# FFN down of layer 1 by seven half-size products, and output products inside the state chain

## What is computed

```python
def conv_ffn(h, p):
    u = dwconv3(h @ p['ffn_up'], p['ffn_conv'])
    ug, uv = jnp.split(u, 2, axis=-1)
    return (jax.nn.silu(ug) * uv) @ p['ffn_down']        # (512, 2816) @ (2816, 1024)

def step(S, inp):                                        # rwkv_scan: both directions, 16 heads
    rt, wt, kt, vt, at, bt = inp
    sa = jnp.einsum('dbhvk,dbhk->dbhv', S, at)
    S = S * wt[..., None, :] + sa[..., :, None] * bt[..., None, :] + vt[..., :, None] * kt[..., None, :]
    y = jnp.einsum('dbhvk,dbhk->dbhv', S, rt) if emit else None
    return S, y
```

## Time and profile before

| | |
|---|---|
| three runs | 2727.85, 2722.11, 2727.54 us (median 2727.54) |
| profiled execution | 2725.52 us, its span 2723.7 us |
| PE busy | 2659.0 us, 98% of the span |
| DVE, ACT, POOL busy | 1398.4, 745.2, 214.9 us |
| granted clock of PE | 0.995 over the span |

### The profile page before, as it was taken

How to read it: one execution, slowest core, us unless ns; L and a number is a source line. 1 busy time by engine, 2 the same in 40 slices (tenths; PEclk the granted TensorE clock), 3 DMA queues, 4 the chain that set the end, 5 groups by cost and what they waited for, 6 DMA issues and landing times.

```text
span 2723.7 us, 61664 instructions
## 1 busy us (share of the span) xinstructions
PE 2659.0 (98%) x27175; PEld 1710.8 (63%) x27175; DVE 1398.4 (51%) x2723; ACT 745.2 (27%) x1566; POOL 214.9 (8%) x184
## 2 busy tenths in 40 slices
PE   7999999999999999999999999999999999999999
PEld 3455555556454545748888544666666677787887
DVE  2677676674222223337778211777877643314541
ACT  3244333442222222111111002443444322311110
POOL 1000000000000002214444000000000000000000
PEclk9999999999999999999999999999999999999999
DMA  7211111111343432344543224212222244356554
GB/s 267 61 48 44 51 51 45 51 48 43 116 116 93 116 111 67 95 130 142 155 124 115 72 72 142 75 53 58 59 60 55 55 124 109 106 153 179 151 149 121
DMA packets 500010, 264.55 MB, mean 97 GB/s; under 512 B 42865, under 2 KB 493889, under 8 KB 499233
## 3 DMA queue, kind: packets, MB, share of 16 engines
q1 hardware_dynamic: 498016, 251.58, 31.9%
q0 software_dynamic: 1728, 9.03, 0.9%
HBM read 255.33 MB, written 5.24 MB: 96 GB/s over the span
## 4 chain that ended last, share of the span: by engine, by line
PE 95%; DVE 2%; DMA 1%; ACT 1%; issue 1%; SPq 0%; DVEq 0%; ACTq 0%
PE psum L515 36%; PE psum L517 15%; PE psum L1190 12%; PE psum L1302 8%; PE psum L549 2%; PE psum L785 2%; PE psum L1019 1%; PE psum L895 1%; PE psum L1007 1%; PE psum L590 1%; PE psum L997 1%; PE psum L758 1%; PE psum L771 1%; PE psum L873 1%; PE psum L731 1%; PE psum L909 1%
## 5 line engine op out<-in xcount | busy, mean ns | idle before, releaser
L515 PE MATMUL psum<-hT,strips 128*128 128x256 f32 (+1 forms) x2234 | 695.0, 462 | 2.4 <-DMA strips<-in_w_in_dram 1.8
L515 PEld LDWEIGHTS psum<-hT,strips 128*128 128x128 f32 x2234 | 414.5, 190 | 228.2 <-issue 192.5
L517 PE MATMUL psum<-hT,strips 128*64 128x512 f32 (+1 forms) x1932 | 403.5, 537 | 4.4 <-DVE arena L2551 2.4
L1302 PE MATMUL psum<-arena,strips 128*128 128x512 f32 (+1 forms) x704 | 227.6, 486 | 0.6 <-DVE arena L2834 0.6
L517 PEld LDWEIGHTS psum<-hT,strips 128*64 128x64 f32 x1932 | 120.9, 137 | 119.4 <-issue 97.6
L1302 PEld LDWEIGHTS psum<-arena,strips 128*128 128x128 f32 x704 | 133.7, 190 | 93.0 <-issue 83.2
L515 PE MATMUL psum<-arena,strips 128*128 128x256 f32 (+1 forms) x416 | 125.9, 461 | 0.9 <-DVE done L2683 0.9
L2834 DVE SCALAR_TENSOR_TENSOR arena<-psum,mod,arena 128x256 f32<-128x256 f32 x24 | 10.9, 481 | 193.7 <-PE psum L1302 193.7
L515 PEld LDWEIGHTS psum<-arena,strips 128*128 128x128 f32 x416 | 78.9, 190 | 45.0 <-issue 36.8
L2216 DVE TENSOR_SCALAR arena<-arena 128x512 f32<-128x512 f32 (+1 forms) x88 | 69.0, 784 | 71.5 <-ACT arena L2068 69.4
L1846 ACT ACTIVATE arena<-psum,arena 128x512 f32<-128x512 f32 (+1 forms) x96 | 58.2, 615 | 151.3 <-DVE arena L2588 151.3
(11 more groups left out here) (306 smaller groups left out, 4110.8 us busy)
## 6 DMA issues: line engine op xcount, KB each, us to landing
strips<-in_w_in_dram SPq DMA_DIRECT2D x152, 512.0 KB, 3.9
strips<-in_ada_w_dram SPq DMA_DIRECT2D x80, 512.0 KB, 4.0
strips<-in_ffn_up_dram SPq DMA_DIRECT2D x46, 512.0 KB, 3.8
strips<-in_ffn_down_dram SPq DMA_DIRECT2D x32, 512.0 KB, 3.9
conv_branch<-in_ffn_up_dram SPq DMA_DIRECT2D x28, 512.0 KB, 4.9
arena<-in_ada_w_dram SPq DMA_DIRECT2D x4, 2048.0 KB, 13.0
strips<-in_w_in_dram SPq DMA_DIRECT2D x32, 256.0 KB, 3.5
strips<-in_a_out_w_dram SPq DMA_DIRECT2D x16, 512.0 KB, 4.5
```

The costliest lines, as they stand in the source:

```text
L515: return pe.matmul(o, lhs, rhs, start=start, stop=stop, skip_group_check=True)
L517: ins = pe.matmul(o[64 * h:64 * h + 64], lhs[:, 64 * h:64 * h + 64], rhs, start=start, stop=stop, skip_group_check=True)
L1302: ins = mm(s.o[:, lo:T], strip[:, b, j, :], hid[:, k, lo:T], k == 0, k == FT - 1)
```

## The change

In layer 1, FFN down is done for pairs of outputs `q`. The first 16 of the 22 blocks of rows go by seven half-size products for each of two groups of eight blocks, summed over the groups in PSUM; the last six blocks (`rest`) are plain matmuls over 512 columns. The pair buffers, the strip sums on POOL and the token sums (now of `hid`) are those of FFN up, with eight more pairs. Layer 2's parameters are turned after the fourth output instead of the third. In both layers the output products of a chunk are issued in the state chain, right behind that chunk's `state_in` and `state_out`; the last chunk's value products stay at the end. The diff, cut:

```diff
--- before.py
+++ after.py
-ALL_PAIRS = LATE_PAIRS + [("up", i) for i in range(1, FT)]
+ALL_PAIRS = LATE_PAIRS + [("up", i) for i in range(1, FT)] + [("down", j) for j in range(D // P)]
...
-PAIR_LOADS = {"gate": 2, "branch": 8, "up": 2}
+FIRST_DOWN = LATE + FT
+SUMMED = 16
+PAIR_LOADS = {"gate": 2, "branch": 8, "up": 2, "down": 2}
...
+        hid_sums = [[arena[:, n:n + 2 * T].rearrange("p (k t) -> p k t", k=4) for n in u] for u in (
+            (AR1_at + 2 * T, after_up), (after_up + 2 * T, after_up + 4 * T),
+            (after_sums + 2 * T, after_sums + 4 * T), (after_up + 6 * T, after_sums))]
+        down_t = arena[:, (n := after_sums + 6 * T):n + T].rearrange("p (j t) -> p j t", j=2)
...
+                fresh = [True, True]
+                def output_bank(i):
+                    if ("y", l, i) not in slots:
+                        take(A, "y", l, i)
+                        fresh[:] = [True, True]
+                    return slots["y", l, i].o
+                def outputs_of_state(c, i):
+                    for d in range(2) if c >= max(c0, 1) else ():
+                        t, back = place(c, d)
+                        for h in range(2):
+                            pe.matmul(output_bank(i)[rows(h), t], GG[rows(h), c, d, :], AR[i % 2][d][rows(h), c, 1, back],
+                                      start=fresh[h], stop=False, skip_group_check=True)
+                            fresh[h] = False
+                def outputs_of_values(c, i):
+                    if c == NCH - 1:
+                        pe.wait_ge(*slots[f"in{c}", l, i].freed)
+                    for d in range(2) if c >= c0 else ():
+                        t, back = place(c, d)
+                        for h in range(2):
+                            ins = pe.matmul(output_bank(i)[rows(h), t], RV[:, c, d, h, :],
+                                            EE[:, 1, c // 4, d, h, c % 4, back], start=fresh[h], stop=True,
+                                            skip_group_check=True)
+                            fresh[h] = False
+                    if c == NCH - 1:
+                        ins.then_inc(slots["y", l, i].full[0], 1)
...
@@ -1169,17 +1188,17 @@
                         state_in(c, i)
                         if c in (1, 2):
                             through_inverse(i, ahead, c + 1)
-                        if c == NCH - 1:
-                            outputs_of_states(i)
-                            if ahead:
-                                diagonal_blocks(i + 1)
+                        outputs_of_state(c, i)
+                        if c == NCH - 1 and ahead:
+                            diagonal_blocks(i + 1)
                         if c > 0:
                             fill(steps, hop)
                         if c < NCH - 1:
                             state_out(c, i)
+                            outputs_of_values(c, i)
                             fill(steps, hop)
                     fill(steps, everything)
-                    outputs_of_values(i)
+                    outputs_of_values(NCH - 1, i)
...
+            def paired_down(q):
+                c, x = slice(0, SEG), slice(SEG, T)
+                ps = down_pairs(q)
+                s, cc = take(Q, "down", 0, 2 * q), take(A, "down11", q)
+                b0 = BANK_P[s.b]
+                u, y, z = PS[:, b0, c], PS[:, b0 + 1, c], PS[:, b0 + 1, x]
+                w2, free = [], []
+                def rest(n):
+                    r = take(G, "rest", n)
+                    pe.wait_ge(*rg.full())
+                    for j in range(FT - SUMMED):
+                        if n == 0:
+                            pe.wait_ge(ev["hid_ready"], SUMMED + j + 1)
+                        ins = mm(r.o, strip[:, rg.last[0], j, :], hid[:, SUMMED + j, :], j == 0, j == FT - SUMMED - 1)
+                        if j == 0:
+                            pay(ins)
+                    ins.then_inc(r.full[0], 1)
+                    owed[0] = rg.free
+                def of_sums(o, j, v, first):
+                    for g, p in enumerate(ps):
+                        pe.wait_ge(ev["strip_sums"], sums_no(p, j + 1))
+                        ins = product(o, strip_sums[p % 2][j], v[g], first and g == 0)
+                        if j == 3:
+                            owed[0] = ev["sums_used"]
+                    return ins
+                for g in range(2):
+                    pe.wait_ge(*pr_w.full(PAIR_LOADS["down"]))
+                    w2.append(pair_w[pr_w.last[0]])
+                    free.append(pr_w.free)
+                    if q == 0:
+                        pe.wait_ge(ev["hid_ready"], 8 * g + 8)
+                    ins = product(u, w2[g][:, 0, 0:4], hid[:, 8 * g:8 * g + 4, c], g == 0)
+                ins.then_inc(ev["down1_ready"], 1)
+                for g in range(2):
+                    ins = product(cc.o[:, c], w2[g][:, 0, 4:8], hid[:, 8 * g + 4:8 * g + 8, c], g == 0)
+                ins.then_inc(cc.full[0], 1)
+                rest(2 * q)
+                if q == 0:
+                    pe.wait_ge(ev["token_sums"], 14)
+                of_sums(y, 0, hid_sums[0], True).then_inc(ev["down5_ready"], 1)
+                pe.wait_ge(ev["down1_kept"], q + 1)
+                if q == 0:
+                    pe.wait_ge(ev["token_sums"], 16)
+                of_sums(u, 1, hid_sums[1], False).then_inc(ev["down6_ready"], 1)
+                pe.wait_ge(ev["down5_kept"], q + 1)
+                if q == 0:
+                    pe.wait_ge(ev["token_sums"], 18)
+                for g in range(2):
+                    pe.wait_ge(ev["strip_sums"], sums_no(ps[g], 4))
+                    product(z, w2[g][:, 1, 4:8], hid_sums[3][g], False)
+                    owed[0] = free[g]
+                pe.wait_ge(ev["down6_kept"], q + 1)
+                if q == 0:
+                    pe.wait_ge(ev["token_sums"], 20)
+                of_sums(u, 2, hid_sums[2], False).then_inc(ev["down7_ready"], 1)
+                of_sums(y, 3, [hid[:, 8 * g + 4:8 * g + 8, x] for g in range(2)], False).then_inc(s.full[0], 1)
+                rest(2 * q + 1)
             def ffn(l, lo):
                 def up(i, j):
@@ -1290,7 +1373,11 @@
                                 for _ in strip_steps(A, up(i, j), lo, hT):
                                     pass
                                 ada_between(4 * i + j)
-                for i in range(KT):
...
-                    if (l, i) == (0, 2):
-                        turn_params(1)
...
+                    elif kind == "down":
+                        sp.dma_start(v[:, q], wcols(a["ffn_down"][0], (n // 2 * 2 + q) * P, 8, n % 2 * 8)).then_inc(pr_w.full(), 16)
...
-                for i in range(KT):
+                for q in range(KT // 2 if l == 0 else 0):
+                    for p in down_pairs(q):
+                        load_pair(p)
+                    for i in range(2 * q, 2 * q + 2):
+                        load(wcols(a["ffn_down"][0], i * P, FT - SUMMED, SUMMED), FT - SUMMED)
...
-                    pool.wait_ge(*slots["down", 0, KT - 1].freed)
+                    pool.wait_ge(*slots["rest", KT - 1].freed)
...
-                    for p in range(LATE + 1, LATE + FT):
+                    for p in range(LATE + 1, len(ALL_PAIRS) + 1):
...
+            def paired_down(q):
+                b0 = BANK_P[slots["down", 0, 2 * q].b]
+                u, y = PS[:, b0, 0:SEG], PS[:, b0 + 1, 0:SEG]
+                act.wait_ge(ev["down1_ready"], q + 1)
+                act.copy(kept_u[q % 2][:, 0], u).then_inc(ev["down1_kept"], 1)
+                act.wait_ge(ev["down5_ready"], q + 1)
+                act.copy(kept_m5[:, q % 2], y).then_inc(ev["down5_kept"], 1)
+                act.wait_ge(ev["down6_ready"], q + 1)
+                act.copy(kept_u[q % 2][:, 1], u).then_inc(ev["down6_kept"], 1)
...
+                def hid_sum(j, g):
+                    v, (t1, t2, t3, t4) = hid[:, 8 * g:8 * g + 8, :], [u[g] for u in hid_sums]
+                    b11, b12, b21, b22 = (v[:, k:k + 4, t:t + SEG] for k in (0, 4) for t in (0, SEG))
+                    o, p, m = ((t1, b12, b11), (t2, b22, t1), (t3, b22, b12), (t4, b21, t2))[j]
+                    tt(o, p, m, SUB).then_inc(ev["token_sums"], 1)
+                def into(k, e, o, done=None):
+                    v = xT[:, k, e * SEG:(e + 1) * SEG]
+                    ins = stt(v, o, mod[:, 0, 5 * KT + k, 1 - e:2 - e], v, MUL, ADD)
+                    if done is not None:
+                        ins.then_inc(done.free, 1)
+                        dve.wait_ge(*done.freed)
+                    else:
+                        ins.then_inc(s_vec, 1)
+                        dve.wait_ge(*order.next())
+                def paired_down(q):
+                    s, cc = slots["down", 0, 2 * q], slots["down11", q]
+                    b0 = BANK_P[s.b]
+                    u, y, z = PS[:, b0, 0:SEG], PS[:, b0 + 1, 0:SEG], PS[:, b0 + 1, SEG:T]
+                    k0, k1 = 2 * q, 2 * q + 1
+                    def rest(n):
```

(91 more changed lines are left out.)

3 lines of the change are left out of this document (added).

## The result

The changed kernel takes 2731.94 us (median of 13 runs, 2728.9 to 2737.12) against 2723.99 us of the kernel before on the same chips; the ratio is 1.0029, 95% interval 1.002 to 1.0037. It is 0.3% slower, where 0.4% faster was forecast. Its profiled execution took 2729.43 us, span 2727.4 us.

A forecast was written before the change was run, and what follows sets the result against it. PE was taken as the bound, busy 2659.0 of 2723.7 us. Terms -14.0 + 1.2 + 4.3 + 1.5 - 1.8 - 1.7 = -10.5 us took 2725.5 to 2715.0 us; range 2707 to 2721, 8 times in 10.

The forecast's parts named there:

- FFN down, 14.0 us less: Layer 1's FFN down on PE: half-size products cut it from 152.46 to 138.5 us, taken in full.
- rival 2: FFN down gives half, each round waiting once or twice at a handover, 1.5 us: 2721.0 us; chance 0.15.
- The wait for c22, 1.2 us: End of FFN up: POOL's new sums slow DVE's taps, so the last product waits 1.2 us once; bounds 0 and 2.
- The issue waits, -1.7 us: PE waits without releaser in bunched small matmuls, 2.6 + 0.8 us: spreading saves half, 1.7 us; from none to all.
- the 6.2 us of L782: PE waits with no releaser at L782: could move either way because the program before them gets longer.
- rival 1: Bunching was the greater cost; waits of L749, L937 and L782 go altogether: 2707.1 us; chance 0.18.
- Half steps, 5.8 us: Half steps wait for DVE's inversion: 4.3 us over seven iterations of layer 1, 1.5 us over seven of layer 2.
- the 0.9 that I had named as a sign of being wrong: Layer 1 half steps: waits of about 0.6 us expected; more than 0.9 us would show the forecast wrong.
- the least gap: Between the end of DVE's inversion and PE's half step: taken as 0.25 us from one layer 2 iteration.
- Chain waits, -1.8 us: Layer 2: value products ahead of `state_in` cover its waits for DVE, 0.25 of 0.29 us, eight times.
- Rival 3: Inversion has no room; all 14 iterations pay their whole shift, 17.2 us, chain gives nothing back: 2729.9 us; chance 0.04.

The follow-up runs named there:

- down_pad112: Kernel before with only the half-size FFN down, plus 28 idle small matmuls (112 PE instructions) ahead of layer 2's parameter turn: 2714.33 us, ratio 0.9963.
- first_part_best: Half-size FFN down alone with 112 idle instructions, POOL's first down-pair strip sums also waiting for DVE's last up-pair c22: 2713.58 us, ratio 0.9956.
- before_pad144: Kernel before plus 36 idle small matmuls (144 PE instructions) ahead of the turn of layer 2's parameters: 2733.37 us, ratio 1.0028.
- hop_less: Changed kernel with 0.57 of a step (0.25 us) less dense work filled into chain gaps where output products now stand: 2725.50 us, ratio 1.0000.
- each alone: Kernel before with only the half-size FFN down: 2722.90 us, ratio 0.9992; with only the output products moved into the state chain: 2741.83 us, ratio 1.0055.
- both_pad112: Changed kernel plus 28 idle small matmuls (112 PE instructions) ahead of the turn of layer 2's parameters: 2728.01 us, ratio 1.0006.
- pad128: Changed kernel plus 32 idle small matmuls (128 PE instructions) ahead of the turn of layer 2's parameters: 2723.32 us, ratio 0.9997.

## Why the prediction was wrong

The forecast was 2715.0 us and faster at 0.90; slower had 0.02, and slower it was. The terms of the sum one by one:

**FFN down, 14.0 us less: right.** 13.8 us in the trace, and 10 to 12 us of net gain in the time once layer 2 is nearly undisturbed (down_pad112: 2725.81 to 2714.33 with 0.6 us of padding). None of the handovers of rival 2 waited.

**The wait for c22, 1.2 us: right**, 1.09 us; first_part_best removes it by its stated cause.

**The issue waits, -1.7 us, from none to all of 3.4: this is the step that failed.** I took the unreleased waits to belong to the bunch of small matmuls and expected the spread order to relieve them. The waits of the diagonal blocks, 2.6 us before, are 5.5 us after. Such waits belong to the boundary of a block of instructions, and the first part, which looked neutral to layer 2, moved all those boundaries. In layer 2 issue waits went from 9.1 to 14.8 us instead of down, one of 3.04 us among them (in layer 1 they stayed at 5.8), and the low clock from 3.4 to 17.1 us. What that clock costs can be estimated from layer 2's chain, 12.0 us longer: issue waits grew by 4.5 us there, other waits by 2.7, and the time in which PE runs by 4.8 us, with 10.3 us more at 1.2 GHz. I had written that the 6.2 us of L782 "can move either way, because the program before them gets longer", and made of it rival 1 alone, on the good side (0.18), and nothing on the bad; the clock had no term at all. That the boundaries do it is shown by before_pad144 (7.6 us lost by 144 idle instructions) and down_pad112 (8.6 us back).

The Trainium skill ("Runtime: NRT & Kernel Launch", section "Instruction fetch mechanics") says that the stream comes in 16 KiB blocks of 256 instructions; every long wait here lies on such a grid. It also says that the cost of a crossing is mostly hidden. The trace agrees for most crossings, 15 waits on the grid for 216 packets in the kernel before; but what is left is not small beside a change of 10 us: 9 to 15 us in layer 2, single waits up to 3.4 us.

**Half steps, 5.8 us: right in mechanism, too small.** 9.3 us in 14 waits: 5.6 in layer 1 for the 4.3 forecast, with one of 1.6 us, over the 0.9 that I had named as a sign of being wrong; and 3.7 in layer 2 for 1.5, where all seven wait, not only the tight ones. I held that the states' products were ahead of the diagonal blocks already and so did not count. But they stood between the last `state_in` and the diagonal blocks; once they are spread, the diagonal blocks follow `state_in` at once and meet DVE in its taps, 0.58 us late at L2542. And the least gap is 0.06, not 0.25 us. hop_less removed all 14 by leaving more dense work behind the diagonal blocks.

**Chain waits, -1.8 us: right.** 2.3 us of `state_in` waits fell to 0.2, and those of `state_out` stayed at 3.7.

**Rivals.** Rival 3 came nearest in the number, slower at 2729.9 us, but by luck: its mechanism (17 us at the half steps, nothing given back by the chain) is not what happened. Its 4 in 100 was far too little for a slower kernel, since a second cost, of several us, had no rival of its own. For both parts together: each alone moves the kernel by -2.1 and +16.8 us, and in the changed kernel they are +7.9; the parts do not add, as each sets where the other's blocks fall; with the blocks at like places (both_pad112) they nearly do.

Open: what of the 9 to 10 us that the second part costs on top of the first is half-step wait and what is fetch and clock behind it in layer 2; the chain of layer 1 alone shows 6.4 to 7.7 us. And why some waits of 2 us are followed by the low clock and others are not.

## What to carry to other kernels

Where a long unrolled program has dense stretches of small instructions, a change of the instruction count anywhere ahead of them can cost or give 0.3%; repeat the kernel with a hundred idle instructions more before a difference of that size is put down to the change. Work that looks idle between an engine and the one that depends on it may be its cover: before moving small work ahead, compare what is left behind it with the time that the other engine's chain needs, and where that engine is when the chain is to start.

## What the runs showed of the hardware

PE's issue waits lie at one place in each 256 of its instructions: 222 of 248 in 13 traces, up to 3.4 us each, and 144 or 112 idle instructions ahead move them to other code (7.6 us lost, 8.6 us won). In such a wait of 3.04 us, with PE busy for 1.96 of 5 us, the granted clock fell to its lower level and stayed there for 10.2 us; in layer 2's chain 10.3 us more of it went with 4.8 us more of running time. Small matmuls of 32x32 cost 0.7 us for 64 records and 128 instructions (pad128).
